# A table of 32 words moves to the end of on-chip memory, and every tile behind it moves 128 bytes down

## The chip, the cores and the metric

The kernel runs on one core of a Trainium2 chip. The metric is the device time of one execution in microseconds (us). It is written in Bass: each engine has its own instruction stream, and the streams meet only at semaphores. The engines are TensorE (matmul, PE in the profile; its weight loads are listed apart as PEld), VectorE (DVE), ScalarE (ACT), GpSimd (POOL) and SyncE (SP), which issues most DMA transfers. SBUF is the on-chip memory that the engines read; it has 128 partitions, and an address below is a byte address within a partition, the same in all 128.

## The reference

Two blocks of two transformer-like layers run one after the other on 256 tokens of width 1024, all in float32. The sizes that matter here are those of the weight products:

```
first_block:  per layer  hn @ w_in,  latent or windowed attention + cross attention to 256 memory rows,
              concat @ w_o,  relu(h @ w_up)**2 @ w_down          (1024 -> 4096 -> 1024)
second_block: layer 0    h @ w_in (1024 -> 2560), convolutions, gated linear recurrence, @ w_out
              layer 1    h @ w_qkv (1024 -> 3072), stick-breaking attention, @ w_out
              both       (silu(h @ w_gate) * (h @ w_up)) @ w_down  (1024 -> 2816 -> 1024)
              both       shift, scale and gate from silu(c) @ ada_w (1024 -> 6144)
```

## The kernel before

A weight product is computed as a *split product*. Both operands are kept as two float32r tiles, a high part (the value rounded) and a low part (the rest), and each block of 128 weights columns by 128 rows costs three matmuls (`product`): high by high (L2153), high weights by low activations (L2154), low weights by high activations (L2155). Each matmul has a weight load of its own before it, on PEld, which may run beside the matmul ahead of it. The matmul reads its *moving* operand from SBUF while the next block of weights is being read from SBUF.

Weights stream through a ring of two slots, `raw`, `w_hi` and `w_lo`, each slot 4096 words (16,384 bytes) in each partition. SP loads a slot into `raw` once it has been split, ScalarE writes `w_hi` (L747), VectorE writes `w_lo` (L1262), TensorE uses the slot. The order of slots is a table (`STREAM`), and all queues follow it. ScalarE may overwrite a slot of `w_hi` once TensorE has used the slot two turns before.

`features` is the common form: for each block of 128 output features and each chunk of 128 inputs it multiplies the weights block by a moving operand of 256 tokens. The moving tiles are `h_both` (the normalized activations, 8 chunks, high and low), `a_both` (the hidden layer of an MLP, up to 32 chunks), `o_hi`/`o_lo` (attention output), `l_hi`/`l_lo` (the recurrence's output) and `m_hi`/`m_lo` (the memory rows, laid over `ada_raw` and the words behind it). Where a product follows a convolution or a shift, the moving operand has 258 columns: `h_wide` (rows 1,032 bytes apart) and `u_hi`/`u_lo` (rows 1,152 bytes apart). `token_rows` turns the roles round: 128 tokens of the activations are the weights of TensorE, and 256 to 512 columns of `w_hi` or `w_lo` move. `keep_warm` (L2238) multiplies one row of `w_hi` by another.

Where things lie follows from the order of the declarations in `build`. SBUF tiles are laid one behind another, each rounded up to 32 bytes. `raw`, `w_hi` and `w_lo` are 32,768 bytes each and `ada_raw` is 8,192, all whole multiples of 512. Behind them comes `line_h` with 48 words (192 bytes), and only then `xT`, `h_wide` (with `h_both` laid over it) and, 32,256 bytes (63 times 512) past the start of `h_wide`, `arena`, which holds `a_both`, `o_hi`, `l_hi`, `u_hi` and the rest. So `h_both`, `a_both`, `o_hi`, `l_hi`, the first row of `u_hi` and, through its end, `m_hi` start 192 bytes past a multiple of 512, counted from the weights. Only `cq_hi`/`ckv_hi` and their low parts begin 256 bytes off that, 448 past.

The weights' blocks keep to multiples of 512 bytes in all slots but one: the second slot of `w_in` has rows of 416 words (1,664 bytes), so a block's start moves on by 128 bytes modulo 512 with each chunk.

`line_h` holds two small tables: `quadrant_sum` (32 words, written once at L1685, read as one operand of 20 matmuls at L2213) and `negsink` (12 words, written at L1686 from `sink`, read at L1706). `line_a` (8 words) and `line_b` (16 words) hold nothing.

Of the kernel before, what the change touches and what calls it, by code (L numbers as in the profile page):

```python
# [24 lines left out]
P = 128  # L25
# [12 lines left out]
SWA_HEADS, SWA_GROUP = 12, 3  # L38
# [132 lines left out]
def build(nc, a, out):  # L171
    ctx = ExitStack()
    with ctx:
        def sb(name, shape, dt=F32):
            return ctx.enter_context(nc.sbuf_tensor(name, shape, dt))
# [6 lines left out]
        w_hi = sb("w_hi", [P, 2, SLOT], F32R)  # L182
        w_lo = sb("w_lo", [P, 2, SLOT], F32R)
        ada_raw = sb("ada_raw", [P, 2, 2, BANK])
        line_h = sb("line_h", [P, 48])
        m_hi = nc.alloc_sbuf_tensor_at("m_hi", [P, KD, T], F32R, offset=nc.sbuf_base - 4 * KD * T)
        xT = sb("xT", [P, KD, T])
        quadrant_sum, negsink = line_h[:, 0:32], line_h[:, 32:32 + SWA_HEADS]
        h_wide = sb("h_wide", [P, 2, KD, T + 2], F32R)
        h_at = nc.sbuf_base - 8 * KD * (T + 2)  # L190
        h_both = nc.alloc_sbuf_tensor_at("h_both", [P, 2, KD, T], F32R, offset=h_at)
# [34 lines left out]
        rsum = sb("rsum", [P, NT, 4])  # L226
        sinkexp = sb("sinkexp", [P, NT, 4])
        sink = sb("sink", [P, SWA_HEADS])

        def at(name, first, shape, dt=F32):  # L230

            return nc.alloc_sbuf_tensor_at(name, shape, dt, offset=arena_at + 4 * first)
# [2578 lines left out]
```

## Time and profile before

| | us |
|---|---|
| median of 3 runs | 1188.12 (1185.74 to 1188.53) |
| the profiled execution, its own time | 1177.91 |
| its span, first to last instruction | 1176.3 |
| PE busy | 1161.4 (99% of the span), 9,553 matmuls |
| PEld busy | 1124.4 (96%) |
| DVE busy | 882.2 (75%) |
| ACT busy | 633.7 (54%) |
| POOL busy | 98.4 (8%) |

The granted clock of TensorE is 1.000 in the mean, its upper level of 2.4 GHz. Matmuls overlap in the record: the duration of one, 270 to 290 ns, reaches from its start to its modelled end, and the next starts some 115 ns after it. A row of a window counts every instruction that touches the window, so a count can be two or three above the number of starts in it.

### The profile page before, as it was taken

How to read it: one execution, taken by the hardware profiler on the slowest of the kernel's cores; microseconds unless marked ns; L12 is line 12 of the kernel's file. 1: busy time of each engine (PE TensorE's matmuls, PEld its weight loads, DVE VectorE, ACT ScalarE, POOL GpSimd, SP SyncE). 2: the span in 40 equal slices, each digit the busy share in tenths (PEclk: the TensorE clock that was granted, in tenths of full speed). 3: DMA queues.
4: the chain of work that ended last, by engine and by line, in shares of the span. 5: the costliest groups of instructions: out<-in, count | busy, mean ns of one | idle time of the engine just before them, and what ended most of it. 6: DMA issues, size and time to landing. Idle time of an engine off the chain costs nothing.

```text
span 1176.3 us, 22917 instructions
## 1 busy us (share of the span) xinstructions
PE 1161.4 (99%) x9553; PEld 1124.4 (96%) x9553; DVE 882.2 (75%) x1177; ACT 633.7 (54%) x853; POOL 98.4 (8%) x147
## 2 busy tenths in 40 slices
PE   8999999999999999999999999999999999999998
PEld 8999999999998999999999999999988779999998
DVE  5876778878766778778889887887777657866543
ACT  6657566633447576633558554343556665543432
POOL 0000001110034001011100001111000000000000
PEclk9999999999999999999999999999999999999999
DMA  8452568887662577787653658868846505576362
GB/s 312 156 179 72 180 220 281 303 309 247 233 233 73 180 252 256 278 317 282 234 181 129 192 159 298 277 233 297 274 147 246 181 5 188 184 262 212 120 198 84
DMA packets 150060, 248.96 MB, mean 212 GB/s; under 512 B 5554, under 2 KB 80923, under 8 KB 149979
## 3 DMA queue, kind: packets, MB, share of 16 engines
q1 hardware_dynamic: 135858, 197.17, 49.8%
q0 software_dynamic: 13952, 50.60, 11.7%
q8 instruction: 59, 0.97, 0.3%
q14 instruction: 23, 0.18, 0.0%
q10 hardware_dynamic: 168, 0.04, 0.0%
HBM read 246.74 MB, written 1.05 MB: 211 GB/s over the span
## 4 chain that ended last, share of the span: by engine, by line
PE 85%; DVE 5%; issue 1%; ACT 1%; DMA 1%; POOL 0%; DVEq 0%; POOLq 0%
PE ps L2153 25%; PE ps L2155 25%; PE ps L2154 25%; DVE w_lo L1262 3%; PE ps L2439 2%; DVE scratch L1764 1%; PE ps L2305 1%; PE ps L2755 1%; ACT w_hi L747 1%; PE ps L2421 1%; DMA ada_raw<-in_l_ada_w 1%; PE ps L2729 1%; PE ps L2408 1%; PE ps L2771 1%; PE ps L2238 0%
## 5 line engine op out<-in xcount | busy, mean ns | idle before, releaser
L1262 DVE TENSOR_TENSOR w_lo<-raw,w_hi 128x2048 fp32r<-128x2048 f32 (+4 forms) x196 | 412.9, 2145 | 94.3 <-ACT w_hi L747 94.0
L747 ACT ACTIVATE w_hi<-raw 128x2048 fp32r<-128x2048 f32 (+4 forms) x196 | 342.1, 1791 | 159.4 <-PE ps L2155 148.8
L2153 PE MATMUL ps<-h_both,w_hi 128*128 128x256 f32 (+1 forms) x1296 | 361.6, 279 | 2.8 <-DVE w_lo L1262 2.1
L2155 PE MATMUL ps<-h_both,w_lo 128*128 128x256 f32 (+1 forms) x1296 | 359.7, 278 | 0.0
L2154 PE MATMUL ps<-h_both,w_hi 128*128 128x256 f32 (+1 forms) x1296 | 359.7, 278 | 0.0
L2153 PEld LDWEIGHTS ps<-h_both,w_hi 128*128 128x128 f32 (+1 forms) x1296 | 242.8, 187 | 4.2 <-issue 3.4
L2155 PEld LDWEIGHTS ps<-h_both,w_lo 128*128 128x128 f32 (+1 forms) x1296 | 244.0, 188 | 0.0
L2154 PEld LDWEIGHTS ps<-h_both,w_hi 128*128 128x128 f32 (+1 forms) x1296 | 242.9, 187 | 0.1
L2153 PE MATMUL ps<-a_both,w_hi 128*128 128x256 f32 x864 | 239.1, 277 | 0.0
L2155 PE MATMUL ps<-a_both,w_lo 128*128 128x256 f32 x864 | 238.6, 276 | 0.0
L2154 PE MATMUL ps<-a_both,w_hi 128*128 128x256 f32 x864 | 238.6, 276 | 0.0
L2153 PEld LDWEIGHTS ps<-a_both,w_hi 128*128 128x128 f32 x864 | 162.2, 188 | 0.2
L2155 PEld LDWEIGHTS ps<-a_both,w_lo 128*128 128x128 f32 x864 | 162.3, 188 | 0.0
L2154 PEld LDWEIGHTS ps<-a_both,w_hi 128*128 128x128 f32 x864 | 162.2, 188 | 0.0
L571 POOL DMA_DIRECT2D ada_raw<-in_l_ada_w x96 | 69.4, 723 | 857.3 <-DVE scratch L1764 857.0
L1764 DVE SCALAR_TENSOR_TENSOR scratch<-ada_raw,silu_c,scratch 128x512 f32<-128x512 f32 x168 | 126.1, 751 | 8.0 <-DMA ada_raw<-in_l_ada_w 0.8
L1155 ACT ACTIVATE a_both<-a_full 128x512 fp32r<-128x512 f32 x18 | 11.4, 632 | 108.0 <-DVE a_full L2028 108.0
L2153 PE MATMUL ps<-h_wide,w_hi 128*128 128x258 f32 x160 | 45.8, 287 | 0.0
L2154 PE MATMUL ps<-h_wide,w_hi 128*128 128x258 f32 x160 | 45.4, 284 | 0.0
L2155 PE MATMUL ps<-h_wide,w_lo 128*128 128x258 f32 x160 | 45.3, 283 | 0.0
L1009 ACT ACTIVATE a_full<-ps 128x512 f32<-128x512 f32 x32 | 19.0, 594 | 47.8 <-PE ps L2155 47.8
L2153 PE MATMUL ps<-w_hi,h_both 128*128 128x512 f32 (+1 forms) x112 | 42.5, 380 | 0.7 <-issue 0.7
(425 smaller groups left out, 1814.6 us busy)
## 6 DMA issues: line engine op xcount, KB each, us to landing
ada_raw<-in_l_ada_w POOLq DMA_DIRECT2D x96, 512.0 KB, 7.0
raw<-in_mlp_w_up SPq DMA_DIRECT2D x32, 1024.0 KB, 6.6
raw<-in_mlp_w_down SPq DMA_DIRECT2D x32, 1024.0 KB, 6.4
raw<-in_l_ffn_w_gate SPq DMA_DIRECT2D x22, 1024.0 KB, 5.5
raw<-in_l_ffn_w_up SPq DMA_DIRECT2D x22, 1024.0 KB, 9.2
raw<-in_l_ffn_w_down SPq DMA_DIRECT2D x16, 768.0 KB, 5.7
raw<-in_l_w_qkv SPq DMA_DIRECT2D x12, 1024.0 KB, 6.7
raw<-in_l_w_in SPq DMA_DIRECT2D x10, 1024.0 KB, 6.3
```

The lines of the kernel that those rows point to most:

```text
L571: pool.dma_start(ada_raw[:, slot, :, :], ada[l][:, 2 * quarter:2 * quarter + 2, group])\
L747: nc.scalar.activation(w_hi[:, s.slot, cut], raw[:, s.slot, cut], ACT.Copy).then_inc(split_hi, 1)
L1009: nc.scalar.activation(full, acc(b if j else FIRST_UP_BANKS[b]).rearrange("p (c t) -> p c t", c=2), ACT.Relu)\
L1262: nc.vector.tensor_tensor(w_lo[:, s.slot, cut], raw[:, s.slot, cut], w_hi[:, s.slot, cut].bitcast(F32), ALU.subtract).then_inc(split_lo, 1)
L1764: ins = nc.vector.scalar_tensor_tensor(ada_sum, w, c, ada_sum, ALU.mult, ALU.add)
L2153: nc.tensor.matmul(to, sh, mh, start=first, stop=False, skip_group_check=True)
L2154: nc.tensor.matmul(to, sh, ml, start=False, stop=False, skip_group_check=True)
L2155: return nc.tensor.matmul(to, sl, mh, start=False, stop=last, skip_group_check=True)
L2305: ins = nc.tensor.transpose(ps[0:ncols, bank, ch * T + t * P:ch * T + (t + 1) * P], src(ch, t), ident[:, :])
L2408: nc.tensor.matmul(s[:, P:3 * P], q[:, P:T], k, start=False, stop=True, skip_group_check=True).then_inc(scores, 1)
L2421: ins = nc.tensor.transpose(ps[:, TURNED_BANKS[lane(hc)], n * P:(n + 1) * P], p[:, n * P:(n + 1) * P], ident[:, :])
L2439: ins = nc.tensor.matmul(ps[:, 6 + g % 2, qt * T + j * HD:qt * T + (j + 1) * HD], p[:, n * P:(n + 1) * P], v, start=j == 0 and n == 0, sto ...
```

## The change

`quadrant_sum` leaves `line_h` for a tile of its own, `quadrant_of`, declared last. `line_h` shrinks from 48 words to 16 and keeps `negsink`.

```diff
-        line_h = sb("line_h", [P, 48])
+        line_h = sb("line_h", [P, 16])
         m_hi = nc.alloc_sbuf_tensor_at("m_hi", [P, KD, T], F32R, offset=nc.sbuf_base - 4 * KD * T)
         xT = sb("xT", [P, KD, T])
-        quadrant_sum, negsink = line_h[:, 0:32], line_h[:, 32:32 + SWA_HEADS]
+        negsink = line_h[:, 0:SWA_HEADS]
 ...
         sink = sb("sink", [P, SWA_HEADS])
+        quadrant_of = sb("quadrant_of", [P, 32])
+        quadrant_sum = quadrant_of[:, :]
```

Every tile declared between them, and `m_hi`, moves 128 bytes down; `raw`, `w_hi`, `w_lo` and `ada_raw` stay. The tiles that lay 192 bytes past a multiple of 512 from the weights now lie 64 past; `cq_hi` and `ckv_hi` lie 320 past. No instruction, wait, semaphore, loop or transfer is added or removed, and the total of SBUF in use is the same.

## Rows read from the trace of the kernel before

**Rows 1.** The page: busy us (share of the span) and instructions.
```profile
PE 1161.4 (99%) x9553; PEld 1124.4 (96%) x9553; DVE 882.2 (75%) x1177; ACT 633.7 (54%) x853; POOL 98.4 (8%) x147
```

**Rows 2.** The page: the chain that ended last, its shares by engine.
```profile
PE 85%; DVE 5%; issue 1%; ACT 1%; DMA 1%; POOL 0%; DVEq 0%; POOLq 0%
```

**Rows 3.** Groups by form, TensorE: line, operation, operands, shapes, count | busy, mean ns.
```profile
L2153 PE MATMUL ps<-h_both,w_hi 128*128 128x256 f32 x1288 | 359.3, 279 | 2.8 <-DVE w_lo L1262 2.1 <-DVE w_lo L1509 0.5
L2153 PE MATMUL ps<-a_both,w_hi 128*128 128x256 f32 x864 | 239.1, 277 | 0.0
L2153 PE MATMUL ps<-o_hi,w_hi 128*128 128x256 f32 x128 | 35.8, 280 | 0.5 <-issue 0.5
L2153 PE MATMUL ps<-l_hi,w_hi 128*128 128x256 f32 x64 | 17.7, 276 | 0.0
```

**Rows 4.** L2153 in single stretches: ns min/median/max, first and last start, form.
```profile
L2153 PE MATMUL ps<-h_both,w_hi x201: 276/276/276, 165.9 to 320.9; 128*128 128x256 f32 x101
L2153 PE MATMUL ps<-a_both,w_hi x256: 276/276/276, 228.8 to 315.5; 128*128 128x256 f32 x128
L2153 PE MATMUL ps<-h_both,w_hi x279: 281/281/290, 1008.8 to 1107.0; 128*128 128x256 f32 x140
L2153 PE MATMUL ps<-a_both,w_hi x18: 281/281/281, 1156.7 to 1162.7; 128*128 128x256 f32 x18
```

**Rows 5.** Stretches of uninterrupted 256-column products: window, length, PE busy (count).
```profile
166.00:322.00 156.00, 156.00 (x1379) 1.00 0.79 275
...
13.00:21.00 8.00, 8.00 (x70) 1.00 1.06 343
21.80:24.80 3.00, 3.00 (x28) 1.00 0.96 350
118.00:163.00 45.00, 45.00 (x384) 1.00 0.53 179
1008.60:1109.80 101.20, 101.20 (x861) 1.00 0.66 217
1156.50:1163.90 7.40, 7.40 (x65) 1.00 0.00 0
```

**Rows 6.** The same columns with all engines (PE, PEld, DVE, ACT, POOL), two stretches.
```profile
1008.60:1109.80 101.20, 101.20 (x861) 101.20 (x860) 67.59 (x63) 42.96 (x37) 4.28 (x6) 1.00 0.66 217
166.00:322.00 156.00, 156.00 (x1379) 156.00 (x1378) 127.89 (x131) 80.55 (x80) 18.82 (x26) 1.00 0.79 275
```

**Rows 7.** L2153 around the second slot of w_in, whose rows are 1,664 bytes apart.
```profile
L2153 PE MATMUL ps<-h_both,w_hi x9: 280/281/281, 22.0 to 24.9; 128*128 128x256 f32 x9
L2153 PE MATMUL ps<-h_both,w_hi x13: 276/276/277, 25.2 to 29.3; 128*128 128x256 f32 x13
L2153 PE MATMUL ps<-h_both,w_hi x15: 276/276/365, 31.9 to 36.7; 128*128 128x256 f32 x8, 128*32 128x256 f32 x7
```

**Rows 8.** Other relations of the two addresses: keep_warm, then products whose weights move.
```profile
L2238 PE MATMUL ps<-w_hi x42: 277/283/469, 643.3 to 858.9; 128*128 128x256 f32 x42
855.39 3.83 PE ps L2238 x32
L2153 PE MATMUL ps<-w_hi,h_both x14: 278/280/388, 346.0 to 350.7; 128*128 128x256 f32 x14
53.00:60.50 7.50, 7.50 (x45) 1.00 0.68 255
61.00:67.90 6.90, 6.90 (x32) 1.00 0.85 304
870.00:882.00 12.00, 12.00 (x54) 1.00 0.56 183
```

**Rows 9.** Groups by form, L2153, 258 columns.
```profile
L2153 PE MATMUL ps<-h_wide,w_hi 128*128 128x258 f32 x160 | 45.8, 287 | 0.0
...
L2153 PE MATMUL ps<-u_hi,w_hi 128*128 128x258 f32 x128 | 36.6, 286 | 0.0
```

**Rows 10.** The moved table's readers at L2213.
```profile
L2213 PE MATMUL ps<-ada_part,line_h x40: 176/203/232, 491.0 to 1110.3; 128*32 128x16 f32 x16, 128*32 128x32 f32 x8, 128*32 128x24 f32 x8, 128*32 128x8 f32 x8
```

## The prediction

> **What bounds the kernel now.** I read the page first. TensorE is busy for 1161.4 of 1176.3 us and no other engine comes near it [rows 1]; the chain that ended last lies on PE for 85% of the span [rows 2]. In the long stretches of weight products nothing waits: in a stretch of 156 us PE is busy for all of it while DVE has 28 us free and ACT 75 [rows 6]. So the time is, to a first order, the number of matmuls times the distance from one start to the next, and the change can act on that distance alone: it adds and removes no instruction.
>
> Then I read the groups by form. Four groups of L2153 have one shape, 256 columns against 128x128 weights, and yet means of 276 to 280 ns [rows 3]. Cut into stretches, the means come apart into two values with nothing between them: 276 ns, minimum, median and maximum, for `h_both` and `a_both` over 150 us, and 281 ns for the same line and the same tiles later on [rows 4]. The spacing goes with it. A window counts each matmul that touches it, so about 2.4 (its 0.28 us over the spacing) come off each count. The fast stretch gives 156 / (1379 - 2.4) = 113.3 ns per matmul, the slow ones 101.2 / (861 - 2.4) = 117.9 and 45 / (384 - 2.4) = 117.9 [rows 5]. The clock is 1.00 in both, and DVE and ACT are less busy in the slow stretch than in the fast one (68 of 101 us against 128 of 156 for DVE) [rows 6], so neither the clock nor traffic of other engines makes the slow spacing. Each kind of stretch holds for hundreds of matmuls with the same tiles at the same addresses. I read that as two self-repeating ways in which the reads of the moving operand and of the next weights fall past each other; which one a stretch gets is decided where it starts.
>
> **D**, below, is the moving operand's address less that of the weights, modulo 512 bytes. For `h_both`, `a_both`, `o_hi`, `l_hi` and `m_hi` it is 192 now and 64 after.
>
> **Does the spacing depend on D?** Three places speak to it.
> - `keep_warm` has D = 0, and its 32 matmuls in a row take 3.83 us, 119.7 ns each [rows 8]: slower than either value at 192.
> - The second slot of `w_in` is an experiment that the kernel makes by itself: its rows lie 1,664 bytes apart, so D runs through 192, 64, 448, 320 with the chunks. The products before it are slow, 28 and 70 in the two windows up to 24.8 us [rows 5]. The slot's first chunk (D = 192) is still at 281 ns; from the second chunk (24.9 us, D = 64) the duration gives way, and from 25.2 us, the third, all 13 of L2153 are at 276 or 277 [rows 7]. After the pause that follows, the rest of the slot, again through all four values, has a median of 276 [rows 7]. So the fast spacing lives at all four values, at least for three matmuls at a time, and the slow one did not survive the step off 192.
> - Where the activations are the weights and `w_hi` moves, `h_both` gives D = 320 and holds a slow stretch too, median 280 ns over 14 [rows 8]; `cq_hi` and `ckv_hi` give D = 64. `cq_hi` (384 columns) takes 7.5 / (45 - 1.9) = 174 ns, which is 116.0 for 256 columns; `ckv_hi` (512) takes 6.9 / (32 - 1.7) = 228, which is 114 [rows 8].
>
> **The change part by part.**
> *The moving operands of the 256-column products.* The slow stretches are the five of [rows 5]: 70 + 28 + 384 + 861 + 65 = 1,408, less 2.4 for each, 1,396 matmuls. At 117.9 - 113.3 = 4.6 ns, of which I take 4.5 (rounded down for the mixed ends of the stretches), they cost 6.3 us. If the slow way doesn't exist at D = 64, all of that goes. Is it on the path? In all five PE runs without a gap (busy equals length), and what comes next would be the ring of weights; in the slow stretch DVE has a third of its time free and ACT more than half [rows 6], and in [rows 4] the same loop ran at 276 ns with DVE at 82%. So nothing is late behind it: -6.3 us. The bounds are wide, since no long stretch at D = 64 with 256 columns is in the trace. From below: -6.3, all fast, in the profiled execution. From above: the nearest rows are 116.0 (`cq_hi`, D = 64) and 119.7 (`keep_warm`, D = 0). The groups of [rows 3] hold 3 x (1288 + 864 + 128 + 64) = 7,032 matmuls, and at 119.7 for all of them it would be 7,032 x 6.4 - 6.3 = +38.7 us. I take -6.3, because the slot of `w_in` has the shape and the tiles of the changed products, which `keep_warm` and `cq_hi` have not.
>
> *The 258-column products*, `h_wide` and `u_hi`, 3 x (160 + 128) = 864 [rows 9]. `u_hi` steps by 128 bytes a chunk and visits all four values of D before and after; `h_wide` steps by 8 bytes and spans 192 to 312 now, 64 to 184 after. The means are 287 and 286 ns for these two very different walks [rows 9]. I take nothing, with 1 ns either way as the bound: 0.9 us.
>
> *The products whose weights move.* D goes from 320 to 448 for `h_both` (6 slots x 2 x 8 chunks x 3 = 288 matmuls of 512 columns in the qkv stage), and from 64 to 192 for `cq_hi` and `ckv_hi` (54 and 36). At 320 a matmul of 512 takes 12 / (54 - 1.7) = 229 ns, at 64 it takes 228 [rows 8]; two values 256 bytes apart make no difference. I take nothing, with 3 ns on 378 matmuls as the bound: 1.1 us.
>
> *The table itself.* The 40 records at L2213 have a median of 203 ns, 8 us if nothing overlapped [rows 10]; they read the same 128 bytes a partition from another place. Nothing, bound 0.2 us. The operations of DVE and ACT on moved tiles, and their transfers, keep their sizes; what they could gain or lose is hidden under PE [rows 6].
>
> Sum: 1177.9 - 6.3 = 1171.6 us against the profiled execution. That one is 10.2 us below the median of the runs, 1188.1. I can't tell from the trace whether the runs without a profile hold more slow stretches. I carry the saving over as it is: 1188.1 - 6.3 = 1181.8 us.
>
> By the Trainium skill ("SBUF — State Buffer", "Who interferes with whom"), the moving operand and the weights come through two independent read ports and TensorE never waits on anyone. Then no address could matter and the sum would be 0. The trace differs: one shape at two spacings, 113.3 and 117.9 ns, and a third, 119.7, where both operands lie in one tile. It doesn't show that D is the reason; so that rule is part of the second rival.
>
> **The rivals.**
> 1. *More is gained.* The 10.2 us between the profiled execution and the runs are slow stretches as well: 10.2 / 0.0045 = 2,270 more matmuls, four in ten of the 5,636 that the profile shows fast. Then D = 64 takes out 16.5 us: 1171.6. For it: the runs differ among themselves by 2.8 us, as stretches that fall one way or the other would make them. Against it: nothing in a profiled execution can show it.
> 2. *The same.* What counts repeats at 256 or 128 bytes, or not at all (192 and 64 are the same modulo 128), both spacings exist at 64 as well, and the start of a stretch decides as before. For it: the slow way also holds at D = 320, which is 64 modulo 256, and 512 columns take the same at 64 and at 320. Against it: the slow stretch of 98 matmuls ended just at the step off 192. Time: 1188.1, with some us either way as the stretches fall (one of 384 matmuls is 1.7 us, the longest of 861 is 3.9).
> 3. *Slower.* D = 64 lies nearer to 0, where the spacing is 119.7, and a long series settles above 113.3. The place is every 256-column product. The one uninterrupted series at D = 64, `cq_hi`, gives 116.0: 7,032 x 2.7 - 6.3 = +12.7 us, 1200.8; if all went to 117.9, 5,636 x 4.5 = +25.4, 1213.5. It decides as soon as more than 1,396 of the 7,032, a fifth, run slow. For it: those two rows. Against it: three matmuls at a time at D = 64 in `w_in` keep 276 ns, and `ckv_hi` has 114 at D = 64.
>
> **How the numbers follow.** Forecast 0.37, more gained 0.15, the same 0.28, slower 0.20. About 0.3% (3.6 us) is what a measurement of this kernel tells from no change. Faster by more: 0.37 x 0.85 + 0.15 + 0.28 x 0.3 = 0.55; slower: 0.20 + 0.28 x 0.3 = 0.28; the rest, 0.17, the same. The likeliest time is 1181.8; its own range is 1178 to 1185. The whole range goes down to 1170, which takes in the first rival, and up to 1201, which takes in the third at the price of `cq_hi` and leaves out its worst half.
>
> **What would show it.** If the mechanism is right, L2153 to L2155 on `h_both`, `a_both` and `o_hi` have a mean of 276 ns in every group, and the stretches that begin near 118 and 1008 us show 113.3 ns; the groups of 258 columns stay near 287 and 286. If the second rival holds, the same two values are there in another share. If the third does, a value other than 276 fills the long stretches of `a_both`. My prediction is wrong if any stretch of over a hundred 256-column products holds 281 ns or more, or if 276 is everywhere and the time has not moved.

## The result and the profile after

The changed kernel takes 1194.67 us (median; 1194.29 to 1198.24 over 4 runs), the kernel before beside it 1188.32 us (1185.74 to 1188.78, 4 runs). The ratio on record is 1.0117, 95% interval 1.007 to 1.0164: slower, where 1181.8 was forecast. The two medians alone are 6.35 us apart, a ratio of 1.0053, and no run of one kernel reaches the runs of the other; how large the loss is depends on how the kernel before falls, as before_again will show. The profiled execution took 1195.0 us, with a span of 1193.4 against 1176.3.

The page after, busy time by engine and the chain's shares by engine:

```profile
PE 1180.5 (99%) x9553; PEld 1142.4 (96%) x9553; DVE 882.7 (74%) x1177; ACT 634.4 (53%) x853; POOL 98.2 (8%) x147
...
PE 86%; DVE 5%; issue 1%; ACT 1%; DMA 1%; POOL 0%; DVEq 0%; POOLq 0%; ACTq 0%
```

Against [rows 1, 2] the counts are the same, DVE, ACT and POOL the same within 1 us, and PE is busy 19.1 us longer. All that was lost, was lost in TensorE's own time.

L2153 of before is L2155 now. The groups by form that answer to [rows 3]:

```profile
L2155 PE MATMUL ps<-h_both,w_hi 128*128 128x256 f32 x1288 | 360.8, 280 | 1.2 <-DVE w_lo L1264 0.7 <-DVE w_lo L1511 0.4
...
L2155 PE MATMUL ps<-a_both,w_hi 128*128 128x256 f32 x864 | 241.2, 279 | 0.0
...
L2155 PE MATMUL ps<-o_hi,w_hi 128*128 128x256 f32 x128 | 35.7, 279 | 0.5 <-issue 0.5
...
L2155 PE MATMUL ps<-l_hi,w_hi 128*128 128x256 f32 x64 | 17.9, 280 | 0.0
```

The means move by 1 to 4 ns, `o_hi`'s goes down. The duration is a label here and not a price: matmuls overlap, and what is paid is the distance between starts. The windows show that, in the columns of [rows 5]:

```profile
118.00:161.00 43.00, 43.00 (x382) 1.00 0.54 186
166.00:322.00 156.00, 156.00 (x1327) 1.00 0.77 271
388.00:425.00 37.00, 37.00 (x316) 1.00 0.57 195
1030.00:1125.00 95.00, 95.00 (x809) 1.00 0.66 212
1130.00:1171.00 41.00, 41.00 (x364) 1.00 0.54 176
```

By the prediction's rule (2.4 off each count) these are 113.3, 117.8, 118.0, 117.8 and 113.4 ns. Both spacings of before are there again at D = 64, at the same clock of 1.00. The stretch at 166 us held 1379 matmuls in 156 us [rows 5] and holds 1327 now. The one at 118 us went the other way: it was slow in [rows 5] and is fast now. L2155 in single stretches, to lay beside [rows 4]:

```profile
L2155 PE MATMUL ps<-o_hi,w_hi x64: 276/276/357, 117.4 to 138.9; 128*128 128x256 f32 x64
L2155 PE MATMUL ps<-h_both,w_hi x186: 279/279/279, 432.5 to 497.9; 128*128 128x256 f32 x186
L2155 PE MATMUL ps<-a_both,w_hi x238: 279/279/279, 502.9 to 586.7; 128*128 128x256 f32 x119
L2155 PE MATMUL ps<-h_both,w_hi x270: 279/280/288, 1029.8 to 1124.8; 128*128 128x256 f32 x135
L2155 PE MATMUL ps<-a_both,w_hi x118: 276/276/276, 1130.0 to 1169.8; 128*128 128x256 f32 x118
```

So each state has its label: 276 ns for the fast spacing at either D; for the slow one 281 at D = 192 and 279 or 280 at D = 64.

From the trace's starts I then added up the distance from each matmul to the next, by kind, in us (the last line is the rest: sums, transposes, attention):

```
kind (count)                          before   after
256 columns, weights from w (7152)     825.3   842.2
258 columns (864)                      106.3   105.5
512 columns, weights move (324)         74.7    76.1
384 columns (54)                         9.6     9.7
256 columns, weights move (144)         17.6    17.3
rest                                   135.5   135.4
```

The first line holds 16.9 us, and the span is 17.1 us longer. A slow matmul is one whose next starts 117 to 119 ns after it. Of some 7,100 in the long series, 1,478 (21%) were slow before and 5,751 (81%) are now. The difference, 4,273, times 117.8 - 113.3 is 19 us, about what PE is longer busy; 2 us of it don't reach the span, since the gaps in PE's work (span less busy) shrank from 14.9 to 12.9 us. Not the two spacings have changed but how much of the kernel runs in which.

### The profile page after: what moved, and what is told of

Its sections match the earlier page's. It is cut to its first block, busy times and chain, and to the rows that moved or that the text cites. A ratio compares the mean times of both kernels' runs of the same rounds, so it can differ in the third digit from the quotient of the medians.

```text
span 1193.4 us, 22917 instructions
## 1 busy us (share of the span) xinstructions
PE 1180.5 (99%) x9553; PEld 1142.4 (96%) x9553; DVE 882.7 (74%) x1177; ACT 634.4 (53%) x853; POOL 98.2 (8%) x147
## 4 chain that ended last, share of the span: by engine, by line
PE 86%; DVE 5%; issue 1%; ACT 1%; DMA 1%; POOL 0%; DVEq 0%; POOLq 0%; ACTq 0%
PE ps L2155 26%; PE ps L2157 26%; PE ps L2156 26%; DVE w_lo L1264 2%; PE ps L2441 2%; PE ps L2307 1%; PE ps L2757 1%; PE ps L2423 1%; ACT w_hi L749 1%; DMA ada_raw<-in_l_ada_w 1%; DVE scratch L1766 1%; PE ps L2731 1%; PE ps L2410 1%; PE ps L2773 1%; PE ps L2240 0%
## 5 line engine op out<-in xcount | busy, mean ns | idle before, releaser
L2155 PE MATMUL ps<-h_both,w_hi 128*128 128x256 f32 (+1 forms) x1296 | 363.0, 280 | 1.2 <-DVE w_lo L1264 0.7
L2155 PEld LDWEIGHTS ps<-h_both,w_hi 128*128 128x128 f32 (+1 forms) x1296 | 242.2, 187 | 2.4 <-issue 1.5
L2155 PE MATMUL ps<-a_both,w_hi 128*128 128x256 f32 x864 | 241.2, 279 | 0.0
L2155 PEld LDWEIGHTS ps<-a_both,w_hi 128*128 128x128 f32 x864 | 162.0, 188 | 0.1
L2155 PE MATMUL ps<-h_wide,w_hi 128*128 128x258 f32 x160 | 45.7, 286 | 0.0
L2155 PE MATMUL ps<-w_hi,h_both 128*128 128x512 f32 (+1 forms) x112 | 42.9, 383 | 0.7 <-issue 0.7
```

The lines of the kernel that those rows point to most:

```text
L2155: nc.tensor.matmul(to, sh, mh, start=first, stop=False, skip_group_check=True)
```

## The experiments

In every one the theories differ in what D does. Spacings that are given to a tenth of a ns are worked out from the starts in the trace.

### Two measuring series: which D has which spacing

**m_map** runs no layer: split products (weights from `w_hi` and `w_lo`, 8 chunks, 2 blocks, 48 matmuls a stretch) from a tile `moving` whose address is shifted, 17 values of D, after seven kinds of start each ("shifted" is two products at D + 32 bytes; the forecast below says 128, but the edit adds 32 bytes). It computes nothing of the reference.

```diff
+            def at(d, c, n=T):
+                o = d // 4 + c * T
+                return moving[:, o:o + n], moving[:, o + 2048:o + 2048 + n]
+            for d in DISTANCES:
+                for s in STARTS:
+                    ...  # pause (PE waits for ACT), walk (9 products at other weight offsets), short_pause, turns, sum, wide, shifted
+                    for q in range(2):
+                        for c in range(KD):
+                            mh, ml = at(d, c)
+                            product(ps[:, 0, q * T:(q + 1) * T], wh[:, c, q * P:(q + 1) * P], ...)
```

> A kernel that only measures: 17 values of D (moving address less weights' address, modulo 512 bytes), 7 kinds of start for each (two pauses, a walk of 9 matmuls through D-128, D-256, D-384, transposes, a float32 sum, 258-column products, a product at D+128), and behind each start 48 split-product matmuls of 256 columns at D with 8 chunks, high and low, as features() makes them. It leaves the reference's computation out; its output is a copy of x. Theory A (two self-repeating spacings, the start decides): at D = 64 and at D = 192 every stretch of 48 is at 113.3 or at 117.8 ns after its first dozen, with nothing between; at D = 192 most starts end at 113.3, at D = 64 most at 117.8; the walk ends at 113.3 at both. Theory B (D alone sets one spacing): each D has one value whatever the start; 64 slower than 192. At D = 0 both expect 119 to 120 ns. Under a repeat of 256 bytes D and D+256 behave alike, under one of 128 bytes 64 and 192 do (then the kernels' difference is chance).

Measured, mean spacing of the last 18 of 48, in ns (D and D + 256 give the same within 0.2 ns, but for three starts of 32, so 17 values come down to these):

```
D mod 256   pause   walk  short_p  turns   sum    wide  shifted
  0, 96     120.0  120.0   120.0   120.0  120.0  120.0  120.0
 16         118.6  118.7   118.6   118.8  116.7  118.6  118.6
 32         117.8  116.7   116.7   116.7  116.9  117.8  120.0
 64         117.8  113.3   117.8   117.8  117.8  117.8  117.8
128         118.4  120.0   120.0   118.6  118.6  118.9  118.8
160         118.9  117.2   117.4   117.3  117.4  117.2  117.5
192         117.8  113.3   113.3   113.3  117.8  113.3  117.8
224         118.2  118.3   118.2   118.2  118.6  118.3  118.5
```

In the trace the state can be read from the first product's line (L241) alone. Here after a pause at D = 0, then pause and walk at D = 64, then pause, walk, short pause and sum at D = 192; behind it a window of the D = 0 stretch (PE busy, count, clock, DMA share, GB/s):

```profile
L241 PE MATMUL ps<-moving,w_hi x11: 283/283/283, 34.1 to 37.7; 128*128 128x256 f32 x11
...
L241 PE MATMUL ps<-moving,w_hi x13: 279/279/279, 168.7 to 173.0; 128*128 128x256 f32 x13
L241 PE MATMUL ps<-moving,w_hi x12: 276/276/276, 175.7 to 179.5; 128*128 128x256 f32 x12
...
L241 PE MATMUL ps<-moving,w_hi x12: 281/281/281, 348.5 to 352.4; 128*128 128x256 f32 x12
L241 PE MATMUL ps<-moving,w_hi x14: 276/276/276, 354.8 to 359.2; 128*128 128x256 f32 x14
L241 PE MATMUL ps<-moving,w_hi x13: 276/276/276, 361.4 to 365.5; 128*128 128x256 f32 x13
L241 PE MATMUL ps<-moving,w_hi x13: 281/281/281, 373.2 to 377.5; 128*128 128x256 f32 x13
```
```profile
34.00:38.00 4.00, 4.00 (x35) 1.00 0.00 0
```

D does set the spacing, with DVE and ACT idle and no transfer under way. The same two spacings exist at 192 and at 64, and what differs is how many starts lead into the fast one: 4 of 7 at 192, 1 of 7 at 64. That is the second rival's mechanism (two ways at 64 too, the start decides) with odds that it took to be equal. Each kind of start was tried once at 64 and 192 and once 256 bytes on, with the same outcome, but always behind the same other stretch, so the 4 and the 1 are counts and not probabilities. The first gaps show the branching: 222 117 117 123 118 113 114 after a short pause at 192, and 221 118 117 118 118 118 at 64.

Could it be the address of the moving tile alone, and not its distance from the weights? A place in the kernels where the roles are turned round answers that: `w_hi` moves, from the same address in all three, and `h_both` gives the weights. D is 320 (64 modulo 256) in the kernel before, 448 (192 modulo 256) in the changed one and 0 in all_0 (below), and the products start every 117.8, 113.3 and 120.0 ns. One line of the product in each, in that order:

```profile
L2155 PE MATMUL ps<-w_hi,h_both x15: 278/279/279, 346.3 to 351.3; 128*128 128x256 f32 x15
L2157 PE MATMUL ps<-w_hi,h_both x15: 276/276/278, 351.1 to 355.9; 128*128 128x256 f32 x15
L2155 PE MATMUL ps<-w_hi,h_both x15: 281/283/283, 357.6 to 362.6; 128*128 128x256 f32 x15
```

**m_fine** is the same with 19 other values, to find out whether a better D lies between.

```diff
-DISTANCES = (0, 16, 32, 64, 96, 128, 160, 192, 224, 256, 288, 320, 352, 384, 416, 448, 480)
+DISTANCES = (8, 24, 40, 48, 56, 60, 68, 72, 80, 136, 144, 152, 168, 176, 184, 188, 196, 200, 208)
```

> The same measuring kernel as before (no part of the reference is computed; its output is a copy of x) at 19 finer distances. Theory A, as the first map left it (a repeat of 256 bytes; 113.3 ns can hold at 64 and at 192 alone, 117.8 too; which comes is the start's doing): 113.3 appears at 64 plus or minus a few bytes and at 192 plus or minus a few, and nowhere else; at 56 to 72 most starts stay at 117 to 118, at 184 to 200 most go to 113.3. Theory D (the exact multiple of 64 is a knife edge between two neighbours, one of which is always fast): one of 60, 68, 188 or 196 shows 113.3 for all seven starts.

Measured: 113.3 nowhere. 56, 60 and 68 hold 117.8 after every start; 72 and 196 hold 121.7 to 122.2, and 136 reaches 122.4 after two of its starts; 48 is at 118.3, 188 at 118.5, 184, 200 and 24 at 120.0. That most starts between 184 and 200 would be fast, as I had expected, is wrong. Among the 36 values tried (28 modulo 256) the fast spacing was found at exactly 64 and 192: 4 bytes to either side it is gone.

### The kernels again

**before_again** and **after_again** are copies of the two kernels: does the split between fast and slow repeat?

```diff
 (no line changed)
```

> The kernel before, once more, for the share of its 256-column products at 117.8 ns in another execution. Theory A with the starts decided anew in each execution: the share differs from the 21% of the first profile, and the span follows at 4.5 ns a matmul: 1176.3 us at 21%, 1187 us at about 55%. Theory C (the profile itself makes the 10 us between 1177.9 and 1188): again some 1177 us with 21%.

> The changed kernel once more. Theory A: the share of slow products is again near 80% (70 to 90%) and the time 1192 to 1198 us, and 0.4 to 1% above the runs of the kernel before on the same chip. Theory C' (it is chance and not D): a share anywhere between 20 and 80%, and times that overlap those of the kernel before.

Measured: 1181.86 us for the one execution of the kernel before (its other runs on that chip: median 1173.96, 1172.6 to 1181.43, 7 runs) and 1194.62 us for the changed one (1190.66 to 1196.49, ratio 1.0152 [1.0107, 1.0197]). The kernel before has 2,806 slow matmuls this time (39%), and they lie elsewhere: the stretch of [rows 4] that was at 276 ns is slow now, the one from 1008 us, slow in [rows 5], is fast (L2153, before_again):

```profile
L2153 PE MATMUL ps<-h_both,w_hi x185: 281/281/281, 166.0 to 231.0; 128*128 128x256 f32 x185
...
L2153 PE MATMUL ps<-h_both,w_hi x192: 276/276/276, 1034.9 to 1099.8; 128*128 128x256 f32 x192
```

The changed kernel repeats itself nearly stretch by stretch: 5,756 slow (81%), span 1193.1. So at 192 the same code falls one way in one execution and the other way in the next, and at 64 four fifths of it fall slow in both. Beside these runs of the kernel before the change costs 20.7 us, in the first comparison 6.3: the changed kernel stays near 1194.6, and the kernel before is what moves.

### Each half of the change alone

**h64_a192** puts the tiles of `h_both` at D = 64 and leaves those of `a_both`, `o_hi` and `l_hi` at 192; **h192_a64** does the opposite.

```diff
 # h64_a192
-        line_h = sb("line_h", [P, 48])
+        line_h = sb("line_h", [P, 16])
 ...
-        quadrant_sum, negsink = line_h[:, 0:32], line_h[:, 32:32 + SWA_HEADS]
+        negsink = line_h[:, 0:SWA_HEADS]
 ...
-        sb("line_b", [P, 16])
+        quadrant_sum = sb("line_b", [P, 48])[:, 0:32]
 # h192_a64
-        lru_shift = sb("lru_shift", [P, 20, 1])
 ...
-        sb("line_a", [P, 8])
 ...
+        lru_shift = sb("lru_shift", [P, 20, 1])      # at the end
```

> Half of the change: h_both, h_wide and m_hi at D = 64, the arena (a_both, o_hi, l_hi, u_hi, cq_hi) back at 192; the table lies in line_b. Theory A by D: stretches of h_both alone start mostly slow, those of a_both that begin anew mostly fast; but a slow stretch of h_both runs on into a_both, whose spacing it sets, since 117.8 ns repeats itself at 192 too. So the time lies between, 1188 to 1195 us, nearer to the change where h_both and a_both follow without a pause. If D = 192 pulls a slow stretch back to fast, a_both is at 113.3 throughout and the time is 1185 to 1190.

> The other half of the change: h_both, h_wide and m_hi stay at 192, the arena (a_both, o_hi, l_hi, u_hi, cq_hi) goes to 64. Theory A: stretches that begin on h_both are fast as often as in the kernel before (some two thirds of the matmuls), those that begin on o_hi or a_both are slow mostly, and where the moving tile passes from 192 to 64 without a pause a fast stretch may fall to slow, as o_hi to h_both did in h64_a192. 1183 to 1193 us, below h64_a192 (1192.4) or equal to it.

Measured: 1192.35 us (1190.99 to 1192.85, ratio 1.014 [1.0101, 1.0179]) and 1193.32 us (1190.97 to 1196.67, ratio 1.0156 [1.0121, 1.019]). The second lies just above what I had expected (1183 to 1193). Each half costs nearly as much as both, so the loss isn't a sum of two halves. One reason stands in the stretch from 117 us, where `o_hi` is followed by `h_both` without a pause. First h64_a192, L2153, then h192_a64, where it is L2152:

```profile
L2153 PE MATMUL ps<-o_hi,w_hi x64: 276/276/357, 117.5 to 139.0; 128*128 128x256 f32 x64
L2153 PE MATMUL ps<-h_both,w_hi x59: 279/279/279, 139.3 to 159.8; 128*128 128x256 f32 x59
```
```profile
L2152 PE MATMUL ps<-o_hi,w_hi x64: 276/276/357, 117.1 to 138.6; 128*128 128x256 f32 x64
L2152 PE MATMUL ps<-h_both,w_hi x60: 281/281/281, 138.9 to 159.8; 128*128 128x256 f32 x60
```

The step from 192 to 64 ends the fast spacing, and so does the step from 64 to 192. A stretch that crossed at the slow spacing (`h_both` to `a_both` at 230 us, both kernels) stayed slow. But a step can also turn slow to fast: at 320.3 us of h192_a64 `a_both` (64) passes to `h_both` (192), and the spacing goes from 117.8 to 113.3 ns (L2152):

```profile
L2152 PE MATMUL ps<-h_both,w_hi x18: 276/276/278, 320.3 to 326.1; 128*128 128x256 f32 x18
L2152 PE MATMUL ps<-a_both,w_hi x7: 279/279/279, 317.8 to 319.9; 128*128 128x256 f32 x7
```

Where D stays the same through the stretch, as in the changed kernel, `o_hi` and `h_both` both keep 276 ns.

### All of them at D = 0

**all_0** gives all these operands D = 0, to see whether the price of the measuring series holds in the kernel.

```diff
-        line_h = sb("line_h", [P, 48])
 ...
-        quadrant_sum, negsink = line_h[:, 0:32], line_h[:, 32:32 + SWA_HEADS]
 ...
+        tables = sb("tables", [P, 48])
+        quadrant_sum, negsink = tables[:, 0:32], tables[:, 32:32 + SWA_HEADS]
```

> The whole kernel with both tables at the end of memory, so that all moving operands stand at D = 0. By the map every 256-column product is at 120.0 ns whatever the start: 7,152 x 120.0 = 858 us against 813 to 829 us in the two profiles of the kernel before, so 1176.3 + 45 = 1221 us, less what the ring of slots hides (1210 to 1222), and hardly any scatter between runs (under 2 us), since no start is left to decide. If D mattered only through 64 against 192, it would be 1175 to 1198.

Measured: 1213.48 us (1212.94 to 1213.63, before 1178.68, ratio 1.0303 [1.0273, 1.0333]). After 6,945 of the 7,152 matmuls the next starts exactly 120 ns later. The window and L2153:

```profile
166.00:320.00 154.00, 154.00 (x1285) 1.00 0.77 270
```
```profile
L2153 PE MATMUL ps<-h_both,w_hi x188: 283/283/283, 165.8 to 233.2; 128*128 128x256 f32 x188
```

154 / 1282.6 is 120.1 ns: the measuring series told the kernel's spacing to 0.1 ns. And the four runs lie within 0.7 us, where the seven of the kernel before on the same chip scatter by 6 and those on another by 9. Where there is one spacing only, there is hardly any scatter. D = 0 isn't the slowest place of the measuring series (72 and 196 are), and for 512 moving columns the order is another: 227 ns at D = 0, 229 at 320, 233 to 235 at 448.

### Turning a slow stretch fast

**m_kick** asks what moves a running stretch from one spacing to the other. At D = 64 and 192 it runs 24 matmuls after a pause (slow in 15 of 15 at 64, fast in 13 of 15 at 192, though the same pause at 192 ended slow in m_map) and 24 after the walk (fast), then one of 14 short disturbances or none, then 48 matmuls. It computes nothing of the reference.

```diff
+                    stretch(d, SETTLE)
+                    kick(d, k)         # e.g. one_128: one matmul with weights from w[..., 32:160]
+                    stretch(d, STRETCH)
+                    kick(d, "nine")
+                    stretch(d, SETTLE)
+                    kick(d, k)
+                    stretch(d, STRETCH)
```

> A measuring kernel (no part of the reference is computed, its output is never written): at D = 64 and 192, a pause, 24 matmuls, a kick of one kind, 48 matmuls; then the walk of nine matmuls over D-128, D-256, D-384, which leaves 113.3 ns at both distances, 24 matmuls, the same kick, 48 matmuls. Theory A: without a kick each stretch keeps its spacing; the walk of nine turns slow into fast; three matmuls at D-128 do it at 192 (117.8, then 114 as in the second slot of w_in) and not surely at 64, where the slot needed six or seven; after a fast stretch the walk changes nothing. A transpose, a float32 matmul or a narrower product between them is a disturbance whose outcome depends on D: at 192 it ends fast, at 64 slow. Theory B' (the spacing belongs to the stretch and not to how it begins): the kicks change nothing.

Measured at D = 64, from slow: one matmul whose weights lie 128 bytes on turns it fast, as do three, six and nine of them, three at 384 bytes and the fp32 matmul; three at 256 bytes don't, nor do a transpose, narrower or wider products or swapped operands. Transpose, narrower, wider and swapped turn a fast stretch slow there; the displaced ones never do. At D = 192 a transpose, 128 or 252 columns and swapped operands turn fast to slow as well (for the transpose I had expected the opposite), 192 and 384 columns don't; no displaced matmul met a slow stretch there. One displaced matmul costs 113 ns, no more than its place. m_kick, second product (L242), before and after one displaced matmul at D = 64, then the same around three at 256 bytes, then around a transpose at D = 192:

```profile
L242 PE MATMUL ps<-moving,w_hi x7: 280/280/280, 51.9 to 54.0; 128*128 128x256 f32 x7
L242 PE MATMUL ps<-moving,w_hi x16: 276/276/276, 54.5 to 59.6; 128*128 128x256 f32 x16
...
L242 PE MATMUL ps<-moving,w_hi x6: 280/280/280, 129.9 to 131.7; 128*128 128x256 f32 x6
L242 PE MATMUL ps<-moving,w_hi x15: 280/280/280, 132.8 to 137.7; 128*128 128x256 f32 x15
...
L242 PE MATMUL ps<-moving,w_hi x8: 276/276/276, 485.2 to 487.5; 128*128 128x256 f32 x8
L242 PE MATMUL ps<-moving,w_hi x15: 281/281/281, 488.4 to 493.3; 128*128 128x256 f32 x15
```

**after_kick** is the changed kernel with 33 such extra matmuls, each into a bank that the next product starts anew; **after_plain** has the same 33 with undisplaced weights; **before_kick** puts the displaced ones into the kernel before.

```diff
+            def extra(s, b, hi, chunk=0):
+                w = ring(w_hi, s.slot, s.kc, s.cols)
+                nc.tensor.matmul(ps[:, b, 0:T], w[:, 0, 32:32 + P], hi[:, chunk, :], start=True, stop=True)   # after_plain: 0:P
 ...
+                    if kick and b:
+                        extra(s, b, hi)
```

> The changed kernel (D = 64) with 33 extra matmuls of 256 columns whose weights lie 128 bytes further on (D = 448 for that one matmul); each is written into a bank that the next product overwrites. Most stand in the second half of a slot: w_o slot 1, every second slot of up, the first of down, the slots of gate_up, ffn_down. Theory A (both spacings repeat themselves, one displaced matmul turns slow into fast and leaves fast as it is): every stretch falls to 113.3 ns at its first extra matmul; the mean over the 7,152 products of 256 columns falls from 117.0 to 113.7 or less, which takes off 7,152 x 3.3 ns = 23 us, less 33 x 0.11 = 4 us for the extra work: 1195 - 19 = 1176 us, 1.5% below the changed kernel. Theory B' (the spacing belongs to the stretch): 1195 + 4 = 1199 us.

> The control: the same 33 extra matmuls with weights that are not displaced (D = 64 like all the others). Every theory: no stretch changes its spacing because of them, and the time is 1195 + 33 x 0.118 = 1199 us. If an extra matmul of any kind resets the reads, it falls like after_kick.

> The kernel before (D = 192) with the same 33 displaced matmuls (D = 64 for those). Theory A: slow stretches of this kernel fall to 113.3 too, as one did in the second slot of w_in; its runs no longer scatter between 1173 and 1189 us but lie within 3 us of 1174 to 1177, 4 us above the best runs without (the extra work), equal to after_kick within 2 us. If the displaced matmul works at D = 64 alone, it is the kernel before plus 4 us with the same scatter.

Measured:

```
              median, us   range             ratio [95%]                 slow matmuls, span
after_kick    1185.36      1184.52-1188.94   1.0085 [1.0058, 1.0112]     2,828 (40%), 1184.0
after_plain   1200.47      1199.82-1200.51   1.0207 [1.0174, 1.024]      6,460 (91%), 1198.2
before_kick   1178.02      1175.47-1182.74   1.0025 [1.0005, 1.0045]     2,299 (32%), 1181.1
before        1174.68      1173.03-1182.16
```

after_kick and after_plain differ only in where 33 of 9,586 matmuls take their weights, and by 15.1 us. So these 15 us are a matter of the state and not of where the moving operands lie. Against the changed kernel without extra matmuls (1194.6) after_kick gains 9.3 us, and 1176 had been expected: the control has 91% slow matmuls and not 81. after_kick around the extra matmul at 190 us, and after_plain at the same place (L2155):

```profile
L2155 PE MATMUL ps<-h_both,w_hi x63: 280/280/280, 168.1 to 190.0; 128*128 128x256 f32 x63
L2155 PE MATMUL ps<-h_both,w_hi x110: 276/276/276, 190.8 to 228.0; 128*128 128x256 f32 x110
```
```profile
L2155 PE MATMUL ps<-h_both,w_hi x63: 279/279/279, 167.7 to 189.8; 128*128 128x256 f32 x63
L2155 PE MATMUL ps<-h_both,w_hi x105: 279/280/280, 190.8 to 227.8; 128*128 128x256 f32 x105
```

But the kick doesn't always work. In after_kick 16 of the 33 met a slow stretch and 8 turned it. It failed after the first 47 matmuls of a stretch at 167.6, 431.7, 498.9 and 759.2 us, and worked 192 further on at 190.3 and 454.5; the failure at 498.9 left `a_both` slow to its end:

```profile
L2155 PE MATMUL ps<-a_both,w_hi x237: 280/280/280, 500.1 to 583.4; 128*128 128x256 f32 x119
```

In before_kick (D = 192) 18 met a slow stretch and 5 turned it; there it worked after the first 47 in three of four places (696.7, 731.0 and 1015.8 us, not 753.6) and failed at each of the six places 96 apart from 1038 to 1096. None of the 32 kicks that met a fast stretch, in the two kernels, turned it slow. before_kick gains nothing, and its runs still scatter by 7 us, which I had expected to end: its 33 extra matmuls at 113 ns are 3.7 us, and it is 3.3 us slower. By its times the kernel before is mostly fast there already; none of those runs has a trace. No version here beats the kernel before.

## Why the prediction was wrong

**The chain to PE, and the spacing as the only thing that can change: right.** 16.9 of 17.1 us lie in the distance between starts of the 256-column products, and nothing became late behind them.

**Two self-repeating spacings, chosen at the start of a stretch: right.** m_map, before_again and the kernels with kicks show it. Whether D matters at all was open; m_map and all_0 settle it. The rule of the Trainium skill ("SBUF — State Buffer", "Who interferes with whom") that TensorE never waits on anyone speaks of what engines do to one another, and DVE and ACT were idle in the measuring series, so nothing here contradicts it. The conclusion that the prediction set beside it, that no address could matter, the runs refute: one shape has 113.3, 117.8, 120.0 and 122.2 ns.

**"If the slow way doesn't exist at D = 64, all of that goes": this step failed.** It does exist there, at 117.8 ns, and it is the likelier of the two: 6 of 7 starts in m_map, 81% of the matmuls in the kernel, against 3 of 7 and 21 to 39% at 192. The term of -6.3 us became +16.9 in the profiled executions. The evidence it rested on, the second slot of `w_in` [rows 7], was read for the wrong cause. The slot walks through 192, 64, 448, 320, and the slow spacing ended in it; I put that down to the arrival at 64. The changed kernel shows the same slot starting *at* 64 and still slow, up to the steps:

```profile
L2155 PE MATMUL ps<-h_both,w_hi x5: 279/279/279, 22.1 to 23.5; 128*128 128x256 f32 x5
L2155 PE MATMUL ps<-h_both,w_hi x5: 278/279/280, 23.5 to 24.9; 128*128 128x256 f32 x5
L2155 PE MATMUL ps<-h_both,w_hi x12: 276/276/277, 25.2 to 29.0; 128*128 128x256 f32 x12
```

The gaps before the starts there are 117 119 117 at D = 64, 119 117 118 at 448, 122 118 117 at 320, 116 114 113 at 192, and 113 from then on at every D. It is the walk over D that turns the state, and "walk" is the one start of m_map that is fast at both 64 and 192. The prediction's own sentence, "the fast spacing lives at all four values, at least for three matmuls at a time", was true. That the slow one lives at 64 too was hardly to be seen, because no long series of this shape at 64 existed; but the kernel before has three products at 64 in that slot, from 24.87 us, and they start 118 and 117 ns apart: the slow spacing did survive the step off 192, and ended on the way through 448 and 320.

**The second rival** (both spacings at 64, the start decides) had the mechanism and gave the time as "the same"; it overlooked that the odds of a start can differ with D. **The third rival** had the sign and its bounds: its threshold was 1,396 slow matmuls, and there are 5,751. Its first price, 1200.8, took 116.0 ns for all of the 7,032 from `cq_hi`; 81% at 117.8 came to more (16.9 against 12.7). Its picture, a spacing that grows towards D = 0, is wrong: 56, 60 and 68 are at 117.8, 72 is at 122.2, 96 at 120.0.

**The test that it named.** "Any stretch of over a hundred 256-column products holds 281 ns or more" would have missed the loss: the slow spacing at 64 is recorded as 279 or 280 ns. The other sign, a mean of 276 ns in every group, did fail (280, 279, 279). The spacing, 117.8 ns, is the thing to test; the duration isn't.

**The small terms.** 258 columns: 0 with 0.9 either way; measured -0.8. Weights that move: 0 with 1.1; measured +1.4 for 512 columns, -0.3 for 256, +0.1 for 384, together +1.2, just past the bound; the reason given, that two values 256 bytes apart make no difference, was drawn from 320 and 64 and says nothing of 448. The table: 0; its 40 records have a median of 203 ns as in [rows 10].

**The 10 us between the profiled execution and the runs.** The kernel before had a median of 1188.3 us in the first comparison and of 1174.0, 1178.7 and 1174.7 in the later ones, and single runs reach from 1172.6 to 1188.8. The first rival took such differences to be the share of slow stretches. before_again fits in direction (1,328 more slow matmuls, PE busy for 5.5 us more, 4.0 us more span, so 3.0 ns for each where the first two profiles give 4.0), and so does all_0, which hardly scatters; at 3.0 to 4.4 ns for each, the runs near 1188 would have 54 to 69% slow matmuls. That is argued, since none of them has a trace, and that something else on another chip or at another hour made them slower isn't excluded.

**Left open.** What in a start picks the spacing, why one displaced matmul turned the stretch after 47 others in three of four places at 192 and in none of four at 64, why after_plain holds more slow matmuls than the changed kernel, and why the two values repeat at 256 bytes. Reads of the two operands that meet in the same part of the memory would fit the repeat, and so would fixed phases of the reads against each other the two states; no run here shows either.

## What to carry to other kernels

Where a profile shows one shape at two spacings with nothing between, count the matmuls in each state before and after, and ask what sets the *odds* of a state, not only whether the state exists. A state that ends where an address passes through several values speaks for the passing as much as for any one of them; series of some 50 matmuls at the fixed address, behind several kinds of start, settle it for the price of one run. If TensorE is the bound, the distance of the moving operand from the weights belongs among the things to measure: from D = 192 to D = 0 it was worth 3% of this kernel (1178.7 to 1213.5 us), and where a fast stretch passed from one tile at 192 to another at 64, or back, the fast spacing ended in all three places traced. It isn't every change of distance that ends it: in the second slot of `w_in`, whose D steps by 128 bytes every three matmuls, it lived on.

## What the runs showed of the hardware

- A 256-column fp32r product with a weight load of its own starts every 113.3 ns or every 116.4 to 122.4 ns (means of 18), depending on the distance of the two operands modulo 256 bytes and on the start, at a granted clock of 1.00 and with DVE and ACT idle. 113.3 was there at 64 and 192 only, and not 4 bytes beside.
- At 64 and 192 there are two stable spacings, with recorded durations of 276 ns (fast) and 279 to 281 ns (slow). Either state held for up to 1,397 matmuls in a row.
- One matmul with its weights 128 bytes on can turn the slow one fast at no cost beyond its own 113 ns (13 of 34 places in the two kernels with such matmuls); one transpose turned fast to slow in all three trials of m_kick, while four in a row left it fast at D = 192 in m_map.
- Runs of one kernel lay between 1172.6 and 1188.8 us, its two profiles had 21% and 39% slow matmuls, and with one spacing only (D = 0) the runs lay within 0.7 us. 33 matmuls out of 9,586 with displaced weights were worth 15 us against 33 whose weights were not displaced.
